# Packed small parameters, weights issued without a wait, and vectors requested later, in a three-block forward pass on one core

## The chip, the core and the metric

The kernel runs as one program on one core of one Trainium2 chip. The metric is the device time of one execution in microseconds (us); less is better. Three executions of the kernel before took 2320.06, 2322.34 and 2329.26 us: the median is 2322.34 us. One more execution was taken by the profiler: it took 2318.49 us, and its span, from the first to the last instruction of the trace, is 2316.6 us.

## What is computed

A sequence of 256 tokens of 1024 numbers, all in float32, passes through three blocks. The change touches the start of the first. Cut to that:

```python
cond = silu(c)
mod = cond @ w_mod + b_mod                      # (1, 6*1024)
sh1, sc1, g1, sh2, sc2, g2 = split(mod, 6)
h = layer_norm(x) * (1 + sc1) + sh1
z = h @ w_in + b_in                             # (256, 6*1024)
a_val, a_gate, sgu, g_a, g_b = split(z, ...)
ya = causal_conv31(a_val * sigmoid(a_gate), conv_w, conv_b)   # depthwise
ya = silu(layer_norm(ya) * ln_a_g + ln_a_b) @ w_a + b_a
u, v = split(gelu(sgu), 2)
yb = (u * (w_s_masked @ layer_norm(v) + b_s)) @ w_b + b_b     # w_s: 8 x 128 x 128
m = sigmoid(g_a) * ya + sigmoid(g_b) * yb
x = layer_norm(alpha * x + g1 * (m @ w_out + b_out)) ...
# then 32 experts with top-4 routing; then a retention and LRU block;
# then a gated linear attention and an S5 block
```

## The kernel before

**Engines and queues.** Each engine runs its own list of instructions in order, and semaphores join them. SyncE (SP) issues the transfers of all big weights. ScalarE (ACT) issues the small parameters and does activations and copies out of PSUM. GpSimd (POOL) issues vectors that are spread over all 128 partitions (`VECTORS`, L538) into two buffers `V`. VectorE (DVE) does norms, additions and the convolution. TensorE (PE) does matrix products and transposes.

**Weights.** All big matrices come in chunks of 1024 rows by 512 columns, 2 MB each, into a ring `W` of six buffers. `plan()` fixes the order: two chunks of `w_mod` for `sc1`, two for `sh1`, then `w_in` in the order ag0, av0, ag1, av1, v0, v1, u0 and so on. SP issues chunk n (L403) when chunk n-6 has been used up; the first six need no such wait.

**The start.** SP issues the constants `K` (L363), then `x` (L364), and then waits for all 19 parameter transfers (L366) and for `w_s` (L367) before the first weight. ACT meanwhile issues those 19 transfers one after the other into `PVR`, `LDT` and `BM` (L1261), and after them `w_s` into `WSR` (L1285). The parameters stand row by row there, so PE turns them with 5 transposes and `w_s` with 8 (helper `turn`, L679); ACT copies the results to `PC` (L1296 to L1301) and `WST` (L1306). ACT applies silu to the 8 columns of `c` (L1303), DVE spreads them to `CB` (L1682) and writes zeros over the masked quarter of `WST` (L1685). DVE then waits for `x` and forms mean, variance and, with a square root on ACT (L337), `RS` (L304 to L316).

**The modulation.** `mod_rows(name)` adds the bias rows `BM` (L649) and multiplies `CB` with each chunk of `w_mod` as it lands (L655). `copy_mod` on ACT copies the result to `MODROW` (L1315), and raises `mod_copied`. `mod_spread(name)` spreads it over all partitions in PSUM (L667). The order on PE is rows sc1, rows sh1, spread sc1, spread sh1. `modulated_norm` on DVE uses spread sc1 for (x - mean) * sc1 (L1695), then spread sh1 for the factor `RS` and the addition (L1703). PE turns the rows of h in 16 transposes over two alternating PSUM banks (L691), ACT copies each bank (`copy_columns`, L354), and then `dense("ag0")` starts (L604).

**After it.** ag and av are column products (L604), all later ones of this stage row products (L616). ACT forms sigmoids of ag (L1327), DVE multiplies (L1733) and runs the 31 steps of the convolution (L1720). The first spread vector is read when v0 and v1 are done (L1667). `WST` is first read by `mix(0)` (L738), after ga1.

The order around the change, on PE:

```python
pe.wait_ge(ev("cond_ready"), 1)
mod_rows("sc1")
mod_rows("sh1")
mod_spread("sc1")
mod_spread("sh1")
h1 = row(HN)
for t in range(TT):
    pe.wait_ge(ev("rows_ready"), NORMED["h1"] + t + 1)
    row_to_columns("h1", t, h1[:, t])
columns_ready("h1")
```

Of the kernel before, what the change touches and what calls it, by code (L numbers as in the profile page):

```python
# [18 lines left out]
ACT = mybir.ActivationFunctionType  # L19

P = 128
T = 256
TT = T // P
D = 1024
# [4 lines left out]
ROW = TT * D  # L29
# [23 lines left out]
R_C, R_AV, R_AG, R_CB, R_BS = 0, 8, 16, 24, 32  # L53
R_CW2, R_CB2, R_GAB, R_GXB, R_LAM, R_BG, R_GLU = 40, 72, 80, 88, 96, 104, 108
R_N0 = 124
N_PARAM = 19
# [89 lines left out]
TRANSPOSES = [("params", 2), ("ws", 2), ("h1", 4), ("yb", 4), ("conv", 4), ("ya", 4), ("m", 4), ("h2", 4),  # L146
# [13 lines left out]
def build(nc, A, out):  # L160
# [20 lines left out]
    with ExitStack() as ctx:  # L181
# [58 lines left out]
        def ev(name):  # L240
            if name not in S:
                S[name] = sem(name)
            return S[name]
# [118 lines left out]
        def _(sp):  # L362
            sp.dma_start(K[:], A["k_const"]).then_inc(const_landed, 16)  # L363
            sp.dma_start(X, A["x"][0].rearrange("(t p) d -> p t d", p=P)).then_inc(x_landed, 16)  # L364

            sp.wait_ge(param_landed, 16 * N_PARAM)  # L366
            sp.wait_ge(ev("ws_landed"), 16)  # L367
# [50 lines left out]
        WSR = half(GB, 0).rearrange("p (g i) -> p g i", g=8)  # L418
        PVR = BIG[:, CV * ROW:CV * ROW + 5 * P].rearrange("p (a b) -> p a b", a=5)
        LDT = BIG[:, CV * ROW + 5 * P:CV * ROW + 5 * P + 2]  # L420
# [112 lines left out]
        def _(pool):  # L533
            for n, (name, off, length) in enumerate(VECTORS):
# [55 lines left out]
        def _(pe):  # L590
# [95 lines left out]
            def row_to_columns(name, t, src):  # L686
                for h in range(2):
                    n = TB[name] + 2 * t + h
                    pe.wait_ge(tp_copied, n - 1)
                    for j in range(4):  # L690
                        ins = pe.transpose(PS[:, 4 + n % 2, j * P:(j + 1) * P], src[:, (4 * h + j) * P:(4 * h + j + 1) * P], ident)  # L691
                    ins.then_inc(tp_ready, 1)
# [19 lines left out]
            pe.wait_ge(param_landed, 16 * N_PARAM)  # L712
            pe.wait_ge(ev("log_dt_ready"), 1)
            turn("params", [[PVR[0:R_N0, 0, :], PVR[:, 1, :], PVR[0:120, 2, :], PVR[:, 3, :]], [PVR[0:80, 4, :]]])
            pe.wait_ge(ev("ws_landed"), 16)
            turn("ws", [[WSR[:, 4 * b + j, :] for j in range(4)] for b in range(2)])
            pe.wait_ge(ev("cond_ready"), 1)
            mod_rows("sc1")
            mod_rows("sh1")
            mod_spread("sc1")  # L720
# [529 lines left out]
        def _(act):  # L1250
# [9 lines left out]
            def param(dst, src):  # L1260
                act.dma_start(dst, src).then_inc(param_landed, 16)  # L1261

            def v128(a):
                return a.rearrange("(r q) -> r q", q=P)

            param(PVR[R_C:R_C + 8, 0, :], v128(A["c"][0]))
            param(PVR[R_AV:R_AV + 8, 0, :], v128(A["b_in"][0, 0:D]))
            param(PVR[R_AG:R_AG + 8, 0, :], v128(A["b_in"][0, D:2 * D]))
            param(PVR[R_CB:R_CB + 8, 0, :], v128(A["conv_b"][0]))
            param(PVR[R_BS:R_BS + 8, 0, :], A["b_s"][0])  # L1270
            param(PVR[R_CW2:R_CW2 + 32, 0, :], A["conv_w_2"].rearrange("j (k q) -> (j k) q", q=P))
            param(PVR[R_CB2:R_CB2 + 8, 0, :], v128(A["conv_b_2"]))
            param(PVR[R_GAB:R_GAB + 8, 0, :], A["gate_a_b_2"])
            param(PVR[R_GXB:R_GXB + 8, 0, :], A["gate_x_b_2"])
            param(PVR[R_LAM:R_LAM + 8, 0, :], v128(A["lru_lambda_2"]))
            param(PVR[R_BG:R_BG + 4, 0, :], v128(A["gla_b_gate_3"][0]))
            param(PVR[R_GLU:R_GLU + 16, 0, :], v128(A["s5_b_glu_3"][0]))
            param(PVR[:, 1, :], A["conv_w"][0, 0:16].rearrange("j (k q) -> (j k) q", q=P))
            param(PVR[0:120, 2, :], A["conv_w"][0, 16:31].rearrange("j (k q) -> (j k) q", q=P))
            param(PVR[0:64, 3, :], A["s5_lam_re_3"][0].rearrange("(a b) p -> a (b p)", b=2))  # L1280
            param(PVR[64:128, 3, :], A["s5_lam_im_3"][0].rearrange("(a b) p -> a (b p)", b=2))
            param(LDT[0:64], A["s5_log_dt_3"][0].rearrange("(a b) -> a b", b=2))
            param(PVR[64:80, 4, :], A["s5_d_3"][0].rearrange("(a b) i -> a (b i)", b=8))
            param(BM, v128(A["b_mod"][0]))
            act.dma_start(WSR, A["w_s"][0].rearrange("g i j -> i g j")).then_inc(ev("ws_landed"), 16)  # L1285

# [5 lines left out]
            for b in range(2):  # L1292
                act.wait_ge(tp_ready, TB["params"] + b + 1)
                n_ = 4 if b == 0 else 1
                if b == 0:
                    act.activation(PC[:, 0, 0:R_N0], PS[:, 4, 0:R_N0], ACT.Copy)  # L1296
                    act.activation(PC[:, 1, :], PS[:, 4, P:2 * P], ACT.Copy)
                    act.activation(PC[:, 2, 0:120], PS[:, 4, 2 * P:2 * P + 120], ACT.Copy)
                    act.activation(PC[:, 3, :], PS[:, 4, 3 * P:4 * P], ACT.Copy).then_inc(tp_copied, 1)
                else:  # L1300
                    act.activation(PC[:, 4, 0:80], PS[:, 5, 0:80], ACT.Copy).then_inc(tp_copied, 1)  # L1301
            act.drain()
            act.activation(pcol(R_C, 8), pcol(R_C, 8), ACT.Silu).then_inc(ev("silu_c_ready"), 1)  # L1303
            for b in range(2):
                act.wait_ge(tp_ready, TB["ws"] + b + 1)
                act.activation(WST[:, 4 * b:4 * b + 4, :], PS[:, 4 + b, :].rearrange("p (k t) -> p k t", k=4),  # L1306
                               ACT.Copy).then_inc(tp_copied, 1)
# [12 lines left out]
            copy_columns(act, "h1", col(HT))  # L1320
            sg = col(U)
# [341 lines left out]
        def _(dve):  # L1663
# [11 lines left out]
            for q in range(4):  # L1675
                dve.tensor_copy(SPREAD[:, q, :], ident[:, 32 * q:32 * q + 1].to_broadcast([P, P]))
            dve.drain()
            dve.wait_ge(param_landed, 16 * N_PARAM)
            dve.tensor_copy(PVR[0:64, 4, :].rearrange("p (b q) -> p b q", b=2),
                            LDT[0:64].unsqueeze(2).to_broadcast([64, 2, 64])).then_inc(ev("log_dt_ready"), 1)  # L1680
            dve.wait_ge(ev("silu_c_ready"), 1)
            dve.tensor_copy(CB, pcol(R_C, 8).unsqueeze(2).to_broadcast([P, KT, 32])).then_inc(ev("cond_ready"), 1)  # L1682
            dve.wait_ge(tp_copied, TB["ws"] + 2)

            dve.memset(WST[64:128, :, 0:64], 0.0).then_inc(ev("wst_ready"), 1)  # L1685
# [22 lines left out]
            modulated_norm(h1, X, "sc1", "sh1", ev("rows_ready"))  # L1708

# [661 lines left out]

# [18 lines left out]
```

## Time and profile before

| | us |
|---|---|
| median of three executions | 2322.34 |
| the profiled execution | 2318.49 |
| its span | 2316.6 |
| TensorE busy with matrix products | 2165.1 |
| VectorE busy | 751.5 |
| ScalarE busy | 468.7 |
| start of the first product with `w_in` (ag0) | 52.17 |

The times of the profile are counted from the start of the span. A busy share over the whole span mixes stages with different limits: the start, up to 52.17 us, is another stage than the one behind it. PE is the engine for products; its weight loads (PEld) lie beside them. Rows of the trace give the start, the duration, the engine (SPq, ACTq and POOLq are issues of transfers), the line, what is written and read, and in square brackets the idle time before it with what ended it. The granted TensorE clock is given as a share of the full 2.4 GHz, so 0.50 is 1.2 GHz.

### The profile page before, as it was taken

To read this page: it belongs to the slowest core of one execution; us is meant where nothing else is said; L and a number is where in the kernel's file an instruction comes from. 1 tells how busy PE (TensorE), PEld (TensorE's weight loads), DVE (VectorE), ACT (ScalarE), POOL (GpSimd) and SP (SyncE) were. 2 spreads that over 40 slices of the span, in tenths; PEclk is the share of its full clock that TensorE was granted. 3 is DMA by queue.
4 is the path that set the end of the run, shared out by engine and by line. 5 is a ranking of instruction groups with operands and counts; after the bars stand their busy time and mean duration, and the time that the engine had idled before them with its cause. 6 is when DMAs were issued, how large, how long until landed. Compare 5 with 4: busy or idle time off the path is not lost.

```text
span 2316.6 us, 30267 instructions
## 1 busy us (share of the span) xinstructions
PE 2165.1 (93%) x11523; PEld 1138.8 (49%) x11524; DVE 751.5 (32%) x1836; ACT 468.7 (20%) x930; POOL 65.4 (3%) x79
## 2 busy tenths in 40 slices
PE   5999998989999998999989998999999999999998
PEld 4844455343333333333333334844565446787873
DVE  1596234212222222222211223232212353988100
ACT  1011102111111111111110111131112215898100
POOL 0000000000000000000000000000000000222000
PEclk9999998999999999999999999999999999999999
DMA  9645557859999999999996799435133323232241
GB/s 345 223 163 181 209 196 285 337 224 417 418 418 418 418 418 381 418 417 418 417 383 265 317 417 384 148 112 200 68 141 133 123 103 125 74 110 74 103 164 42
DMA packets 158855, 591.31 MB, mean 255 GB/s; under 512 B 5323, under 2 KB 6927, under 8 KB 125887
## 3 DMA queue, kind: packets, MB, share of 16 engines
q1 hardware_dynamic: 152512, 573.08, 63.2%
q0 software_dynamic: 4384, 16.40, 2.0%
q8 instruction: 51, 0.84, 0.1%
q10 hardware_dynamic: 1887, 0.81, 0.1%
q14 instruction: 21, 0.17, 0.0%
HBM read 589.23 MB, written 1.05 MB: 255 GB/s over the span
## 4 chain that ended last, share of the span: by engine, by line
PE 74%; DMA 15%; DVE 5%; ACT 3%; DVEq 2%; issue 1%; ACTq 0%; SPq 0%
PE PS L616 22%; PE PS L922 13%; DMA W<-in_w_gu 13%; PE PS L604 10%; PE PS L945 6%; PE PS L1129 4%; PE PS L631 4%; PE PS L869 2%; PE PS L958 2%; PE PS L1202 1%; DVE BIG L1924 1%; PE PS L886 1%; DVE BIG L1928 1%; DMA W<-in_w_mod 1%; DVEq L1927 1%
## 5 line engine op out<-in xcount | busy, mean ns | idle before, releaser
L616 PE MATMUL PS<-W,BIG 128*128 128x512 f32 x1152 | 501.0, 596 | 5.0 <-DVE BIG L2358 2.9
L922 PE MATMUL PS<-W,BIG 128*64 128x512 f32 x2048 | 451.8, 595 | 21.0 <-DMA W<-in_w_gu 20.9
L616 PEld LDWEIGHTS PS<-W,BIG 128*128 128x128 f32 x1152 | 219.4, 191 | 277.2 <-issue 270.5
L922 PEld LDWEIGHTS PS<-W,BIG 128*64 128x64 f32 x2048 | 142.1, 137 | 313.0 <-issue 270.8
L945 PE MATMUL PS<-W,BIG 128*64 128x512 f32 x1024 | 228.8, 600 | 7.0 <-ACT BIG L1408 6.9
L604 PE MATMUL PS<-BIG,W 128*128 128x256 f32 x1024 | 222.2, 379 | 1.4 <-ACT BIG L354 1.4
L604 PEld LDWEIGHTS PS<-BIG,W 128*128 128x128 f32 x1024 | 194.2, 190 | 28.9 <-ACT BIG L354 1.9
L1922 DVE TENSOR_SCALAR BIG<-PS 128x512 f32<-128x512 f32 (+1 forms) x38 | 24.7, 650 | 379.6 <-PE PS L922 355.9
L945 PEld LDWEIGHTS PS<-W,BIG 128*64 128x64 f32 x1024 | 71.1, 138 | 144.0 <-issue 126.3
L1403 ACT ACTIVATE BIG<-BIG 128x512 f32<-128x512 f32 x32 | 20.2, 632 | 488.9 <-DVE BIG L1922 488.9
L1129 PE MATMUL PS<-BIG,W 128*128 128x256 f32 x512 | 118.3, 385 | 0.5 <-ACT BIG L1563 0.5
L1129 PEld LDWEIGHTS PS<-BIG,W 128*128 128x128 f32 x512 | 95.6, 192 | 15.6 <-issue 3.5
L1917 DVE COPY BIG<-PS 128x256 f32<-128x256 f32 x32 | 13.6, 425 | 260.1 <-PE PS L958 258.7
L1720 DVE SCALAR_TENSOR_TENSOR BIG<-BIG,PC 128x255 f32<-128x255 f32 (+29 forms) x240 | 95.4, 465 | 3.8 <-issue 0.5
L631 PE MATMUL PS<-W,BIG 128*128 128x512 f32 x192 | 82.9, 592 | 0.0
L827 PE MATMUL PS<-BIG 128*64 128x512 f32 x256 | 62.5, 610 | 4.3 <-issue 4.3
L1411 ACT ACTIVATE BIG<-PS 128x512 f32<-128x512 f32 x32 | 19.1, 598 | 232.1 <-PE PS L945 232.1
L958 PE MATMUL PS<-BIG 64*128 64x256 f32 x512 | 63.9, 389 | 0.8 <-ACT BIG L1411 0.8
L958 PEld LDWEIGHTS PS<-BIG 64*128 64x128 f32 x512 | 47.0, 186 | 30.9 <-issue 26.8
L631 PEld LDWEIGHTS PS<-W,BIG 128*128 128x128 f32 x192 | 36.5, 190 | 45.9 <-issue 45.9
L2111 DVE TENSOR_TENSOR X<-X,PS 128x512 f32<-128x512 f32 x12 | 8.0, 686 | 128.1 <-PE PS L631 67.5
L869 PE MATMUL PS<-W,BIG 128*32 128x256 f32 x768 | 45.6, 398 | 3.0 <-DVE BIG L1932 3.0
(460 smaller groups left out, 1963.2 us busy)
## 6 DMA issues: line engine op xcount, KB each, us to landing
W<-in_w_gu SPq DMA_DIRECT2D x128, 2048.0 KB, 17.3
W<-in_w_dn SPq DMA_DIRECT2D x64, 2048.0 KB, 19.1
W<-in_w_in SPq DMA_DIRECT2D x24, 2048.0 KB, 15.1
W<-in_w_mod SPq DMA_DIRECT2D x12, 2048.0 KB, 9.6
W<-in_gla_w_in SPq DMA_DIRECT2D x10, 2048.0 KB, 7.9
W<-in_s_w_in SPq DMA_DIRECT2D x8, 2048.0 KB, 8.9
W<-in_s_w_glu SPq DMA_DIRECT2D x8, 2048.0 KB, 8.0
W<-in_w_out SPq DMA_DIRECT2D x6, 2048.0 KB, 8.3
```

The source lines that it names most:

```text
L604: ins = pe.matmul(ps[:, m // 2, (m % 2) * T:(m % 2 + 1) * T], slot(c0 + i)[:, k, m * P:(m + 1) * P], lhs(i * KT + k), start=i + k == 0, st ...
L616: ins = pe.matmul(ps[:, t, :], lhs(i * KT + k)[:, t * P:(t + 1) * P], w[:, k, :], start=i + k == 0, stop=last_chunk and k == KT - 1)
L631: ins = pe.matmul(ps[:, t, :], lhs(i * KT + k)[:, t * P:(t + 1) * P], w[:, k, :], start=i + k == 0, stop=i == 1 and k == KT - 1)
L827: ins = pe.matmul(PS[hh[h], 3, :], G[:, t, :], H2[:, t, h * CH:(h + 1) * CH], start=t == 0, stop=t == TT - 1, skip_group_check=True)
L869: ins = pe.matmul(PS[qq[q], g, 0:T], XETX[:, k, :], gu_w(k)[:, g * D + q * T:g * D + (q + 1) * T], start=False, stop=k == KT - 1, skip_gro ...
L886: ins = pe.matmul(PS[qq[q], 2, T:2 * T], ACTTX[:, k, :], dn_w(k)[:, q * T:(q + 1) * T], start=k == 0, stop=k == KT - 1, skip_group_check=True)
L922: ins = pe.matmul(PS[hh[h], g, :], XET[:, k, :], gu_w(k)[:, g * D + h * CH:g * D + (h + 1) * CH], start=False, stop=k == KT - 1, skip_grou ...
L945: ins = pe.matmul(PS[hh[h], 2, :], ACTT[:, k, :], dn_w(k)[:, h * CH:(h + 1) * CH], start=k == 0, stop=k == KT - 1, skip_group_check=True)
L958: ins = pe.matmul(PS[:, 4 + q, t * T:(t + 1) * T], SC[r, t * P:(t + 1) * P], YE[r, (q % 2) * T:(q % 2 + 1) * T], start=False, stop=False, ...
L1129: ins = pe.matmul(PS[:, 5, part * T:(part + 1) * T], slot(c0)[:, k, m * P:(m + 1) * P], lhs(k), start=k == 0, stop=k == KT - 1, skip_group ...
L1720: ins = dve.scalar_tensor_tensor(cv[:, k, lag:], ya[:, k, 0:T - lag], pcol(r), cv[:, k, lag:], ALU.mult, ALU.add)
L1922: dve.tensor_scalar(GT[:, w], PS[:, 0, w], 7.0, None, ALU.min).then_inc(clipped, 1)
```

## The change

- The parameters are laid out on the host side in one array `k_params` of 128 x 640 numbers in the turned order that `PC` has (`log_dt` repeated 64 times). ACT issues three transfers: `PC`, `BM`, and `x`, which moves here from SP. The 18 small transfers, `PVR`, `LDT`, the 5 transposes, ACT's five copies and DVE's copy of `LDT` are gone.
- SP issues the weights right behind `K`, with no wait.
- `w_s` is laid out turned as well. ACT issues it straight into `WST`, behind the copies of h1. Its 8 transposes and two copies are gone. DVE waits for it behind `modulated_norm` and writes the zeros there.
- POOL waits for `mod_copied` 2 (sc1 and sh1 copied) before its first vector.
- PE spreads sc1 before the rows of sh1.

```diff
-            sp.dma_start(X, A["x"][0].rearrange("(t p) d -> p t d", p=P)).then_inc(x_landed, 16)
-
-            sp.wait_ge(param_landed, 16 * N_PARAM)
-            sp.wait_ge(ev("ws_landed"), 16)
...
         def _(pool):
+            pool.wait_ge(ev("mod_copied"), 2)
...
-            pe.wait_ge(param_landed, 16 * N_PARAM)
-            pe.wait_ge(ev("log_dt_ready"), 1)
-            turn("params", [[PVR[0:R_N0, 0, :], PVR[:, 1, :], PVR[0:120, 2, :], PVR[:, 3, :]], [PVR[0:80, 4, :]]])
-            pe.wait_ge(ev("ws_landed"), 16)
-            turn("ws", [[WSR[:, 4 * b + j, :] for j in range(4)] for b in range(2)])
+            pe.wait_ge(param_landed, 32)
             pe.wait_ge(ev("cond_ready"), 1)
             mod_rows("sc1")
+            mod_spread("sc1")
             mod_rows("sh1")
-            mod_spread("sc1")
             mod_spread("sh1")
...
-            param(PVR[R_C:R_C + 8, 0, :], v128(A["c"][0]))
...
-            param(BM, v128(A["b_mod"][0]))
-            act.dma_start(WSR, A["w_s"][0].rearrange("g i j -> i g j")).then_inc(ev("ws_landed"), 16)
+            act.dma_start(PC[:], A["k_params"].rearrange("p (a r) -> p a r", a=5)).then_inc(param_landed, 16)
+            act.dma_start(BM, A["b_mod"][0].rearrange("(r q) -> r q", q=P)).then_inc(param_landed, 16)
+            act.dma_start(X, A["x"][0].rearrange("(t p) d -> p t d", p=P)).then_inc(x_landed, 16)
...
+            act.wait_ge(param_landed, 32)
             act.activation(pcol(R_C, 8), pcol(R_C, 8), ACT.Silu).then_inc(ev("silu_c_ready"), 1)
...
             copy_mod("sc1")
             copy_mod("sh1")
             copy_columns(act, "h1", col(HT))
+            act.dma_start(WST, A["w_s"].rearrange("j (g i) -> j g i", g=8)).then_inc(ev("ws_landed"), 16)
...
-            dve.wait_ge(tp_copied, TB["ws"] + 2)
-
-            dve.memset(WST[64:128, :, 0:64], 0.0).then_inc(ev("wst_ready"), 1)
             dve.wait_ge(x_landed, 16)
...
             modulated_norm(h1, X, "sc1", "sh1", ev("rows_ready"))
+            dve.wait_ge(ev("ws_landed"), 16)
+
+            dve.memset(WST[64:128, :, 0:64], 0.0).then_inc(ev("wst_ready"), 1)
```

## Rows read from the trace of the kernel before

**Rows 1.** Busy time by stage: us, busy (instructions) of each engine, clock, DMA, GB/s

```profile
0.00:52.00 52.00, 25.18 (x333) 19.78 (x334) 10.35 (x25) 9.24 (x19) 1.46 (x6) 0.93 0.95 340
52.00:108.00 56.00, 55.83 (x258) 48.98 (x259) 26.61 (x66) 5.82 (x11) 0.00 (x0) 1.00 0.65 234
108.00:192.00 84.00, 84.00 (x209) 38.22 (x208) 80.10 (x185) 6.61 (x5) 2.12 (x4) 1.00 0.51 176
```

**Rows 2.** The chain that ended last, 0 to 60 us: start, duration, what

```profile
9.34 4.13 DMA BIG<-in_w_s
...
18.26 21.31 DMA W<-in_w_mod
...
39.61 1.96 PE PS L655 x64
41.57 1.94 PE PS L667 x8
...
46.34 0.75 DVE BIG L1703
...
47.80 3.69 PE PS L691 x16
...
51.52 0.61 ACT BIG L354
```

**Rows 3.** Timeline of the start: start, duration, engine, line, what, count

```profile
0.73 0.38 SPq L363 DMA_DIRECT2D K<-in_k_const  x1
...
16.53 0.29 DVE L1682 COPY BIG<-PC 128x256 f32<-128x256 f32 x1 [3.75 <-ACT PC L1303]
...
18.20 2.47 DVE L304 BATCH_NORM_STATS2 ST<-X 128x6 f32<-128x512 f32 x4
...
21.30 0.20 ACT L337 ACTIVATE SD<-VE 128x2 f32<-128x2 f32 x1 [2.49 <-DVE VE L309]
...
21.80 3.64 PE L655 MATMUL PS<-W,BIG 128*32 128x128 f32 x64 [4.28 <-DMA W<-in_w_mod]
...
27.23 3.62 PE L655 MATMUL PS<-W,BIG 128*32 128x128 f32 x64 [1.20 <-DMA W<-in_w_mod]
...
30.93 0.38 ACT L1315 ACTIVATE MISC<-PS 128x256 f32<-128x256 f32 x1 [9.42 <-PE PS L655]
...
34.19 3.56 PE L655 MATMUL PS<-W,BIG 128*32 128x128 f32 x64 [2.98 <-DMA W<-in_w_mod]
```

**Rows 4.** Transfers, 0 to 60 us: rate in 40 slices of 1.5 us, three issues

```profile
GB/s 0 242 378 387 316 330 293 195 162 31 255 412 406 386 389 386 385 388 388 393 386 389 384 388 386 389 389 386 388 384 386 389 385 388 389 384 388 385 386 388
...
X<-in_x SPq DMA_DIRECT2D x1, 1024.0 KB, 7.2
V<-in_b_in POOLq DMA_DIRECT2D x2, 512.0 KB, 8.3
K<-in_k_const SPq DMA_DIRECT2D x1, 528.0 KB, 3.4
```

**Rows 5.** Transfers from 13.5 to 39.6 us, all queues together

```profile
DMA packets 4666, 9.45 MB, mean 362 GB/s; under 512 B 64, under 2 KB 64, under 8 KB 4664
```

**Rows 6.** PE alone in short stretches: us, busy (instructions), clock, DMA, GB/s

```profile
34.10:35.50 1.40, 1.31 (x28) 0.51 1.04 383
...
41.50:43.50 2.00, 2.00 (x13) 1.00 1.06 389
47.70:48.70 1.00, 0.90 (x4) 0.54 1.04 383
```

**Rows 7.** Timeline: the next work of ACT and DVE, and V's first use

```profile
66.29 1.57 ACT L1327 ACTIVATE BIG<-PS,PC 128x256 f32<-128x256 f32 x4 [12.87 <-PE PS L604]
...
80.16 1.66 DVE L1733 SCALAR_TENSOR_TENSOR BIG<-PS,PC,BIG 128x256 f32<-128x256 f32 x4 [31.10 <-PE PS L604]
...
125.38 1.22 DVE L1667 TENSOR_TENSOR BIG<-PS,V 128x1024 f32<-128x1024 f32 x1
```

**Rows 8.** Line L538, all transfers of spread vectors: issue to landing

```profile
DMA to landing us min/median/max: 3.8/6.9/13.0
```

More of the change, by code:

```diff
@@ L55 @@
 R_N0 = 124
-N_PARAM = 19
 def constants():
@@ L142, in plan @@
     return units
-TRANSPOSES = [("params", 2), ("ws", 2), ("h1", 4), ("yb", 4), ("conv", 4), ("ya", 4), ("m", 4), ("h2", 4),
+TRANSPOSES = [("h1", 4), ("yb", 4), ("conv", 4), ("ya", 4), ("m", 4), ("h2", 4),
               ("xn", 4), ("q", 4), ("k", 4), ("yr", 4), ("hg", 4), ("kend", 1), ("og", 8), ("hs", 4)]
@@ L417, in build @@
         MODROW = MISC[:].rearrange("p (j c) -> p j c", c=T)
-        WSR = half(GB, 0).rearrange("p (g i) -> p g i", g=8)
-        PVR = BIG[:, CV * ROW:CV * ROW + 5 * P].rearrange("p (a b) -> p a b", a=5)
-        LDT = BIG[:, CV * ROW + 5 * P:CV * ROW + 5 * P + 2]
         MA, MB = half(9, 0), half(9, 1)
@@ L688, in row_to_columns @@
                     n = TB[name] + 2 * t + h
-                    pe.wait_ge(tp_copied, n - 1)
+                    if n >= 2:
+                        pe.wait_ge(tp_copied, n - 1)
                     for j in range(4):
@@ L1258, in half_copies @@
                                    PS[:, 4 + n % 2, :].rearrange("p (k t) -> p k t", k=4), ACT.Copy).then_inc(tp_copied, 1)
[L1260 to L1264, printed above, removed]
-            param(PVR[R_C:R_C + 8, 0, :], v128(A["c"][0]))
[L1267 to L1283, printed above, removed]
-            param(BM, v128(A["b_mod"][0]))
-            act.dma_start(WSR, A["w_s"][0].rearrange("g i j -> i g j")).then_inc(ev("ws_landed"), 16)
+            act.dma_start(PC[:], A["k_params"].rearrange("p (a r) -> p a r", a=5)).then_inc(param_landed, 16)
+            act.dma_start(BM, A["b_mod"][0].rearrange("(r q) -> r q", q=P)).then_inc(param_landed, 16)
+            act.dma_start(X, A["x"][0].rearrange("(t p) d -> p t d", p=P)).then_inc(x_landed, 16)
             def unit_act(name, dst, func, **kw):
@@ L1289, in unit_act @@
                 free_unit(act.activation(dst, unit_ps(name), func, **kw), name)
[L1292 to L1302, printed above, removed]
+            act.wait_ge(param_landed, 32)
             act.activation(pcol(R_C, 8), pcol(R_C, 8), ACT.Silu).then_inc(ev("silu_c_ready"), 1)
[L1304 to L1307, printed above, removed]
             act_std(act)
@@ L1677, in _ @@
             dve.drain()
-            dve.wait_ge(param_landed, 16 * N_PARAM)
-            dve.tensor_copy(PVR[0:64, 4, :].rearrange("p (b q) -> p b q", b=2),
-                            LDT[0:64].unsqueeze(2).to_broadcast([64, 2, 64])).then_inc(ev("log_dt_ready"), 1)
             dve.wait_ge(ev("silu_c_ready"), 1)
             dve.tensor_copy(CB, pcol(R_C, 8).unsqueeze(2).to_broadcast([P, KT, 32])).then_inc(ev("cond_ready"), 1)
-            dve.wait_ge(tp_copied, TB["ws"] + 2)
-            dve.memset(WST[64:128, :, 0:64], 0.0).then_inc(ev("wst_ready"), 1)
             dve.wait_ge(x_landed, 16)
@@ L2369, with packed, put @@
           "s5_b_im_3", "s5_c_re_3", "s5_c_im_3", "s5_d_3", "s5_w_glu_3", "s5_b_glu_3", "s5_w_out_3", "final_norm_3"]
+PACKED = ["c", "b_in", "conv_w", "conv_b", "b_s", "conv_w_2", "conv_b_2", "gate_a_b_2", "gate_x_b_2", "lru_lambda_2",
+          "gla_b_gate_3", "s5_b_glu_3", "s5_lam_re_3", "s5_lam_im_3", "s5_log_dt_3", "s5_d_3"]
+def packed(a):
+    rows = np.zeros((P, 5, P), np.float32)
+    def put(at, r, v):
+        v = np.reshape(v, (-1, P))
+        rows[r:r + v.shape[0], at] = v
+    put(0, R_C, a["c"])
+    put(0, R_AV, np.reshape(a["b_in"], -1)[0:D])
+    put(0, R_AG, np.reshape(a["b_in"], -1)[D:2 * D])
+    put(0, R_CB, a["conv_b"])
+    put(0, R_BS, a["b_s"])
+    put(0, R_CW2, a["conv_w_2"])
+    put(0, R_CB2, a["conv_b_2"])
+    put(0, R_GAB, a["gate_a_b_2"])
+    put(0, R_GXB, a["gate_x_b_2"])
+    put(0, R_LAM, a["lru_lambda_2"])
+    put(0, R_BG, a["gla_b_gate_3"])
+    put(0, R_GLU, a["s5_b_glu_3"])
+    put(1, 0, a["conv_w"][0, 0:16])
+    put(2, 0, a["conv_w"][0, 16:31])
+    put(3, 0, a["s5_lam_re_3"])
+    put(3, 64, a["s5_lam_im_3"])
+    put(4, 0, np.repeat(np.reshape(a["s5_log_dt_3"], (64, 2)), 64, axis=1))
+    put(4, 64, a["s5_d_3"])
+    return np.reshape(np.transpose(rows, (2, 1, 0)), (P, 5 * P))
 def kernel(**inputs):
@@ L2377 @@
     arrays, A = {}, {}
-    for name, a in [(n, inputs[n]) for n in INPUTS] + list(constants().items()):
+    laid = {n: inputs[n] for n in INPUTS if n not in PACKED or n == "b_in"}
+    laid.update(constants(), k_params=packed({n: np.asarray(inputs[n]) for n in PACKED}))
+    for name, a in laid.items():
+        if name == "w_s":
+            a = np.reshape(np.transpose(np.asarray(a)[0], (2, 0, 1)), (P, 8 * P))
         if name in ("s5_b_re_3", "s5_b_im_3"):
```

## The prediction

> **What bounds the kernel now.** I read the stages first [rows 1]. Behind 52 us TensorE is busy for 55.83 of 56 us and then for 84.00 of 84 us, while the transfers move 234 and 176 GB/s, well under the 386 to 393 of the start [rows 4]: from there on products set the pace, and nothing in this stretch counts from time zero. Before 52 us PE is busy for 25.18 of 52 us, most of it waiting. So the change is worth what it takes off the start of the first product, 52.17 us in the table, and everything behind it should move as one piece.
>
> Then the chain of waits of that start [rows 2]. It runs through the landing of `w_s` at 13.47 us (9.34 + 4.13), which frees SP to issue weights; through the weight stream up to 39.57 us; and through a tail of 12.6 us from there to 52.17: rows of the last chunk 1.96, spread sc1 1.94, DVE's first pass up to 46.34, half of its second pass 1.4 (46.34 to 47.80), transposes 3.69, the last copy 0.61. The timeline [rows 3] shows that the parameters' own work is no part of it beyond the issue: `CB` is ready at 16.82 us and the statistics are read from 18.20, while the first chunk lands only at 21.8.
>
> **Parts 1 and 2, parameters packed and weights at once: the last w_mod chunk lands earlier.** The parameters' issues go, and with them SP's wait. The bytes stay, and decide. The first bytes of `K`, issued at 0.73 us, come near 2.1 us: the slice from 1.5 to 3 moved 242 GB/s times 1.5 us = 0.36 MB, which is 0.94 us at 388 GB/s, a rate of many later slices [rows 3, 4]. What has to pass before the fourth chunk is in: `K` 0.54 MB, `PC` 128 x 640 x 4 = 0.33, `BM` 0.02, `x` 1.05, four chunks 8.39, together 10.33 MB. A transfer is not in when its own bytes' worth has moved, as later ones run beside it: between 13.5 us and the landing at 39.6 the queues moved 9.45 MB for those 8.39 [rows 5], so 1.06 MB more. I add the same: 11.4 MB at 388 GB/s = 29.4 us, so the fourth chunk lands at **31.4 us** against 39.57, 8.2 us earlier. Bounds: without the 1.06 MB it is 28.7; with twice as much, for two hardware queues where before was one, 34.1. I take the middle because it is the same stream through the same queue.
>
> The vectors (two times 0.5 MB) are out of that sum, since POOL now waits. It has only their issues in its queue, and the first reader is at 125.38 us [rows 7]; with the slowest landing of 13.0 us [rows 8] an issue near 34 lands by 47. So the wait costs nothing by itself. But they now run beside the chunk of ag0. That one lands 5.4 us behind the fourth (2.1 MB at 388), near 36.8; with 1.05 MB of vectors ahead of it, near 39.5. The first product wants it at 41.6 by the sum below: covered, by about 2 us. Without that cover it costs up to 2.7 us.
>
> The removed 13 transposes, 7 copies and DVE's one copy all lie before 21.8, on no path: nothing. The new path to `CB` is the landing of `PC`, silu, 0.29 us for `CB` [rows 3]. `PC` is a third of `x`'s size, and `x` took 7.2 us and `K` 3.4 [rows 4], so it lands between 4 and 9 us. The first chunk is in at 2.1 + (0.54 + 1.40 + 2.10 + 0.4)/0.388 = 13.5 us (with 0.4 MB more for what runs beside it, an estimate below the 1.06 of the fourth). `CB` is hidden, with 3 us or more to spare; later than 13.5 it would cost one for one only until PE catches up.
>
> **x behind the parameters on ACT.** DVE's statistics and the root take 3.3 us (18.20 to 21.5 [rows 3]), and ACT's square root stands in ACT's queue before the copy of sc1. That copy is wanted at about 22.6 us. The spread vectors, on a queue of their own beside SP's, took 13.0 us at most [rows 8]; by that `x`, issued near 1.8, lands by 15, and the root is done by 18.5. Hidden. The trace has no other case of a megabyte on ACT's queue, so this is the weakest cover; it is rival 2.
>
> First what the row shows: with three queues at work (SP, ACT, POOL) the total was 378 to 387 GB/s in the slices from 3 to 6 us, no more than the one queue's 388 later [rows 4]. A rule stands beside it that speaks against a part of this change: the Trainium skill, "DMA: Bandwidth & Descriptors", section "Issuing engines are not separate DMA queues", says that transfers from different engines end on the same 16 DMA engines and interleave, so that another issuer saves only its issuing time. By that rule `x` on ACT takes its 2.7 us from the weights, as my sum has it; if the queues added up, `PC` and `x` would cost nothing and the gain would be 3.6 us more.
>
> **Part 3, spread sc1 before rows sh1: a shorter tail.** The second chunk lands near 2.1 + (1.94 + 4.19 + 0.43)/0.388 = 19.0. Rows of a chunk take 3.64 us at the lower clock [rows 3], so they are done at 22.7, the copy (0.38 and two hand-overs, 0.5) at 23.2, the spread by 25.2 at the high clock (1.94) or 27.1 at the low one (twice that). The third chunk lands near 25.6, so its rows end at 29 to 31.3, ahead of the fourth. DVE does its first pass (2.8 us) meanwhile. So of the tail go 1.94 for spread sc1 and 2.8 for the first pass; what appears is what they hid: the copy of sh1 0.5 and spread sh1, about 1.85 (8 matmuls like spread sc1). New tail: 1.96 + 0.5 + 1.85 + 0.05 + 1.46 (half of the second pass) + 3.7 + 0.65 = 10.2 us against 12.6: **2.4 us** less. Bounds: 1.3 more if the transposes run at the high clock (below), and 3.5 less if the fourth chunk's rows and the spread still run at the low one (3.64 for 1.96, and 1.85 again).
>
> The clock is why these bounds stand. PE's 64 matmuls of a chunk took 3.6 us for each of the first three chunks [rows 3] and 1.96 for the fourth [rows 2]: 1.2 GHz, then 2.4. The granted clock reads 0.51 at 34.1 and 1.00 at 41.5 [rows 6]; before 34 the column reads 1.00, but the spacing of 57 ns is that of the lower level. It rose while PE was active with gaps of 1.2 to 3.3 us, and was down again at the transposes (0.54 at 47.7) behind an idle stretch of 2.6 us. In the new order PE works from 19 to 31 us with shorter gaps than before, thus the fourth chunk's rows should be at the high level as now. The gap before the transposes shrinks to 1.5 us. At the high level the 4 banks would go at the pace of ACT's copies, 0.45 + 4 x 0.65 = 3.05 us instead of 4.35: the 1.3 above. The Trainium skill, "TensorE: Matmul & The Clock Gate", section "The HAM clock gate", says that the array halves its rate after an idle stretch and that the point at which it changes varies from run to run; the trace's 0.54 behind 2.6 us of idling agrees. By that rule the shorter gap makes a fall less likely, and the sum would be the one with 1.3 more.
>
> **Part 4, w_s later.** Issued at about 41 us on ACT (0.6 us, next work of ACT before the change 14 us behind the start of ag0, [rows 7]), it lands within 4.1 [rows 2] to 13.0 us [rows 8], by 54 at the latest. DVE waits for it with the convolution queued behind; its next work stands 28 us behind the start of ag0, at 69.5 in the new time. The zeros take 0.5 us at most. `mix(0)` reads `WST` over 100 us later. Nothing. Without that cover each us of delay would go onto the convolution, which keeps DVE busy for 80.10 of 84 us [rows 1].
>
> **Sum.** 8.2 + 2.4 = 10.6 us, first product at about 41.6. Against the profiled execution: 2318.5 - 10.6 = 2307.9. That execution is 3.9 us below the median of the three; against the median it is 2322.3 - 10.6 = **2311.7 us**, 0.46% less. What is late next is the product chain itself.
>
> **Rivals.**
> 1. *The clock stays up over the transposes*: 11.9 us, 2310.4. For it: the gap of 1.5 instead of 2.6 us. Against it: the transposes of h1 are at the low level in the trace, though spread sc1 and spread sh1 just before them were at the high one.
> 2. *x is held behind the weights* (the other side). If ACT's queue got its turn only when SP's six chunks are through, `x` would land at 2.1 + (0.54 + 12.58 + 0.35 + 1.05)/0.388 = 39.5 us. Then statistics 3.3, root and copy of sc1 0.7, spread 1.94, both chunks' rows with their bias 4.8, copy 0.5, spread 1.85, and the end of the tail 5.9: first product at 58.5, 6.3 us later than now: 2328.6. It is slower than before once `x` lands after 33 us. Against it: POOL's vectors, on another queue than SP's, landed in at most 13.0 us beside full streams [rows 8]. The Trainium skill, the same DMA page, section "Queues, rings and completion order", says that each DMA engine takes turns between its queues; that agrees with this row.
> 3. *The landing slips, or the low clock stays*: twice the overshoot (2.7 us), the vectors beside ag0's chunk (up to 2.7), or the low clock in the last rows and the spread (3.5). Each alone leaves 7 to 8 us, two together 4 to 5: 2314.4 to 2318. For it: `w_mod`'s third chunk came 7.0 us behind the second (27.23 to 34.19 [rows 3]) where the others took 5.4, so such slips occur in this stream.
> 4. *The change does not reach the end*: the gain in the start is given back behind it, in a stage bound by transfers. Against it: no stage of rows 1 behind 52 us waits for a transfer that counts from zero. Time: 2318 to 2322.
>
> **How the numbers follow.** Forecast 45%, rival 1 25%, rival 3 20%, rival 2 5%, rival 4 5%. Three executions of before lie 9.2 us apart, so a median of three can be off by 2 to 3 us by itself. The range must leave 2 in 10 out: low, rival 1 with 4 us of scatter and a shorter landing (28.7 is 2.7 us below the forecast), 2305; high, rival 3 whole and 1 us of scatter, 2319. What a measurement can tell from no change is 0.5%, 11.6 us, just above the forecast's 10.6. So the forecast gives "faster" in about 4 cases of 10, rival 1 in 5.5 of 10, rival 3 hardly (0.18 + 0.14 + 0.02 = 0.34, some 0.38 with the possibility that the stream overshoots less); slower by 11.6 us is out of reach even of rival 2 (2%); the rest, 0.60, is within.
>
> **What would show it.** Right: the fourth chunk's rows at about 31.4 us, spread sc1 finished before they start, first L604 at 41 to 42, and every later stage the same length as before. `x`: statistics before 18 us. Part 3 is wrong if DVE's first pass still stands behind the fourth chunk; part 4 if DVE's line of the zeros waits past 69 us. The clock shows in the duration of the 64 matmuls (1.96 or 3.6) and of the transposes. The prediction is wrong above all if the product stages behind 52 us change their length, which the rows give no reason for.

## The result and the profile after

Five executions of the changed kernel have a median of 2305.66 us (2303.67 to 2306.96), five of the kernel before, on the same chip, 2320.31 us. The ratio is 0.993, with a 95% interval from 0.9913 to 0.9946: 14.7 us less by the medians, where the prediction said 10.6 and gave the larger chance, 0.60, to a change of less than 0.5%. The whole interval lies beyond 0.5%. The time is inside the range (2305 to 2319), at its lower edge.

The profiled execution of the changed kernel took 2306.96 us, the slowest of its five, and its span is 2304.8 us, 11.8 less than before. Its chain of waits at the start (start, duration, what; it answers to rows 2):

```profile
0.73 0.38 SPq L362
...
9.72 20.97 DMA W<-in_w_mod
30.69 0.04 issue
30.73 2.00 PE PS L648 x64
...
32.75 0.39 ACT MISC L1268
...
33.19 2.01 PE PS L660 x8
...
35.22 0.75 DVE BIG L1651
...
36.69 0.67 PE PS L685 x4
...
38.12 0.64 PE PS L685 x4
...
39.92 20.12 PE PS L597 x92
```

L648, L660, L1651, L685 and L597 are here what L655, L667, L1703, L691 and L604 were. The landing of `w_s` and DVE's first pass are no longer in the chain. The fourth chunk lands at 30.7 us instead of 39.6, and the first product starts at 39.92 instead of 52.17: 12.25 us earlier, 8.88 from the landing and 3.37 from the tail.

The timeline of the same stretch shows the work that the prediction held to be covered by other work (start, duration, engine, line, what, idle before; it answers to rows 3 and 7):

```profile
6.53 0.29 DVE L1633 COPY BIG<-PC 128x256 f32<-128x256 f32 x1 [1.05 <-ACT PC L1260]
...
10.99 2.47 DVE L303 BATCH_NORM_STATS2 ST<-X 128x6 f32<-128x512 f32 x4 [4.16 <-DMA X<-in_x]
13.19 3.64 PE L648 MATMUL PS<-W,BIG 128*32 128x128 f32 x64 [5.57 <-DMA W<-in_w_mod]
...
24.78 2.72 DVE L1643 SCALAR_TENSOR_TENSOR BIG<-X,MV,PS 128x512 f32<-128x512 f32 x4 [10.29 <-PE PS L660]
...
47.09 0.48 DVE L1659 MEMSET BIG<- 64x512 f32 x1 [9.15 <-DMA BIG<-in_w_s]
67.92 1.66 DVE L1684 SCALAR_TENSOR_TENSOR BIG<-PS,PC,BIG 128x256 f32<-128x256 f32 x4 [20.34 <-PE PS L597]
```

`CB` is ready at 6.8 us, 6 us ahead of the first chunk's rows. `x` has landed at 11, so the statistics are done long before the copy of sc1. DVE's first pass runs at 24.8, ahead of the fourth chunk. The zeros of `WST` end at 47.6, and DVE's next work is at 67.9.

Behind the start these two traces are alike. The products of ag and av take 55.52 us in both, and the first product of v0 starts at 95.44 against 107.69. From the first product to the end of the span it is 2264.9 us against 2264.4.

### The profile page after: what moved, and what is told of

It is laid out like the page before. It is cut to its first block, busy times and chain, and to the rows that moved or that the text cites. A ratio compares the mean times of both kernels' runs of the same rounds, so it can differ in the third digit from the quotient of the medians.

```text
span 2304.8 us, 30211 instructions
## 1 busy us (share of the span) xinstructions
PE 2159.5 (94%) x11510; PEld 1133.0 (49%) x11511; DVE 752.1 (33%) x1835; ACT 464.1 (20%) x922; POOL 65.4 (3%) x79
## 3 DMA queue, kind: packets, MB, share of 16 engines
HBM read 589.29 MB, written 1.05 MB: 256 GB/s over the span
## 4 chain that ended last, share of the span: by engine, by line
PE 74%; DMA 15%; DVE 5%; ACT 3%; DVEq 2%; issue 1%; SPq 0%; ACTq 0%
PE PS L609 22%; PE PS L912 14%; DMA W<-in_w_gu 13%; PE PS L597 10%; PE PS L935 6%; PE PS L1119 4%; PE PS L624 4%; PE PS L859 2%; PE PS L948 2%; PE PS L1192 1%; DVE BIG L1875 1%; PE PS L876 1%; DVE BIG L1879 1%; DMA W<-in_w_mod 1%; DVEq L1878 1%
## 5 line engine op out<-in xcount | busy, mean ns | idle before, releaser
L597 PE MATMUL PS<-BIG,W 128*128 128x256 f32 x1024 | 222.2, 379 | 1.5 <-ACT BIG L353 1.5
L597 PEld LDWEIGHTS PS<-BIG,W 128*128 128x128 f32 x1024 | 194.2, 190 | 29.0 <-ACT BIG L353 1.9
L1873 DVE TENSOR_SCALAR BIG<-PS 128x512 f32<-128x512 f32 (+1 forms) x38 | 24.7, 650 | 382.2 <-PE PS L912 356.5
```

Of the source, the lines that this page charges most:

```text
L597: ins = pe.matmul(ps[:, m // 2, (m % 2) * T:(m % 2 + 1) * T], slot(c0 + i)[:, k, m * P:(m + 1) * P], lhs(i * KT + k), start=i + k == 0, st ...
L1873: dve.tensor_scalar(GT[:, w], PS[:, 0, w], 7.0, None, ALU.min).then_inc(clipped, 1)
```

## The experiments

The kernel before ran 58 times beside them, on three chips with medians of 2320.1, 2320.3 and 2321.0 us: 2314.9 to 2329.0 us, median 2320.3. These executions differ more than the changes that I wanted to price, so a time below is read with its interval, and the trace of one execution of each kernel gives the places. "Landing" is the start of the fourth `w_mod` chunk's rows, "first product" the start of ag0. The low and the high level of the clock are 1.2 and 2.4 GHz; the 64 matmuls of a chunk's rows take 3.64 us at the one and 1.95 at the other, and a time between the two is a change on the way.

### The changed kernel again (r1_after_again)

No edit.

> The changed kernel again. The theory (the gain is the earlier start of the first product, 12.25 us in the first trace, and nothing behind it) expects a ratio of 0.9945 to 0.995, a difference of the medians of 11.5 to 12.5 us, and the first product again at 39.9 us. The rival (something behind the start gains 2 to 4 us more, which the first profiled pair happened not to show) expects a difference of 14 to 16 us, a ratio of 0.993 to 0.994.

Six executions: median 2309.06 us, ratio 0.9943 (0.9927 to 0.9959), 12.0 us less than the 2321.02 beside it. Together with the first five, eleven executions have a median of 2306.8 us, **13.5 us or 0.58% less** than the 58 of before. So the first ratio was a little lucky, and 10.6 a little short. The first product came at 41.60 and not at 39.9 as expected. The reason stands in PE's timeline and its stretches (us, busy, clock, DMA, GB/s):

```profile
30.77 3.62 PE L648 MATMUL PS<-W,BIG 128*32 128x128 f32 x64 [3.10 <-DMA W<-in_w_mod]
34.87 1.99 PE L660 MATMUL PS<-MISC,TAB 128*128 128x256 f32 x8 [0.48 <-ACT MISC L1268]
```

```profile
25.30:27.30 2.00, 1.94 (x68) 1.00 1.05 387
30.80:32.80 2.00, 2.00 (x40) 0.51 1.04 383
```

The landing is the same to 0.04 us. The clock had been at 2.4 GHz for the third chunk's rows and was at 1.2 for the fourth's, behind 3.10 us of waiting for weights; in the first trace it stayed up over 3.11 us of the same waiting. Of the traces with the new start (r1_after_again, c1_old_order, d1_pool_free, x1_x_first, h1_small_head and the first), five show the low level there, for all or most of it, with 3.3 to 3.6 us, and one 1.96. My sum had the high level; the low one stood in rival 3 only.

### Only SP's waits out (b1_weights_free)

```diff
-            sp.wait_ge(param_landed, 16 * N_PARAM)
-            sp.wait_ge(ev("ws_landed"), 16)
```

> The kernel before with SP's two waits ahead of the weights taken out, nothing else. If only bytes count, x, the parameters, w_s and the vectors (1.05 + 0.3 + 0.5 + 1.05 MB) now share the queues with the weights: fourth w_mod chunk at 2.1 + (12.0 + 0.7)/0.388 = 34.7 us, first product at about 47.3, 4.9 us earlier than 52.17. The rival, that the many small parameter transfers are held up beside full streams, expects the parameters complete only behind 20 us and a gain under 3 us.

Landing at 36.07 and first product at 48.32 us, 1.4 and 1.0 later than by bytes alone. Median of ten 2318.75, ratio 0.9983 (0.9970 to 0.9995). PE's timeline:

```profile
23.82 1.97 PE L677 MATMUL PS<-K,BIG 128*128 128x128 f32 x8 [5.65 <-DMA BIG<-in_w_s]
...
26.30 2.74 PE L653 MATMUL PS<-W,BIG 128*32 128x128 f32 x64
```

`w_s`, 0.5 MB, was issued at 9.55 us on ACT and landed at 23.8: 14.3 us beside SP's stream, where it took 4.1 without one [rows 2]. PE stood behind it with the first chunk landed (17.8 us by the trace of its transfer; the second came at 24.7, the third at 30.1), and caught up just before the fourth. So the rival about held-up small transfers has the mechanism right (the last parameter came at 16.6 instead of 12.5 us) but not the amount, as it expected 20. Taking the waits out alone is worth 3.9 us at the first product. The medians differ by 2.3 us only; ag and av took 57.26 us here and not 55.52, so that v0 starts 2.1 us earlier than in the first trace. The rest of the landing's gain is in the bytes taken out of its way.

### Spread sc1 behind the rows again (c1_old_order)

```diff
             mod_rows("sc1")
-            mod_spread("sc1")
             mod_rows("sh1")
+            mod_spread("sc1")
             mod_spread("sh1")
```

> The changed kernel with spread sc1 put back behind the rows of sh1. The fourth chunk should land at 30.7 us as before. If the order is worth spread and first pass (4.75 us less the 2.4 that they hid), the first product comes at 42.2 us with the transposes at the high clock, and at 43.5 if the longer idle stretch ahead of them brings the low clock back. The rival, that the order is worth nothing because PE keeps up anyway, expects 39.9.

Landing 30.82, first product 44.78 us; median of seven 2311.46, ratio 0.9954 (0.9938 to 0.9969). The chain (start, duration, what):

```profile
30.82 3.33 PE PS L648 x64
34.14 1.94 PE PS L660 x8
36.10 0.75 DVE BIG L1643
...
38.92 0.75 DVE BIG L1651
...
40.38 3.73 PE PS L685 x16
```

From the landing to the first product it is 13.96 us with 3.33 for the rows; r1_after_again had 10.83 with 3.62. Less the rows, that is 10.6 against 7.2: the order is worth **3.4 us**. Of them 1.2 are the clock (4.40 us from the first transpose to the first product, against 3.24). The 16 transposes take 3.73 us here behind an idle stretch of 2.6 us, as in the kernel before [rows 2], and run at the high level behind 1.5 us in the new order. The branch of the expectation with the low clock (43.5 us) was right, once the rows' 1.4 us are taken off.

### The new order alone (e1_order_alone)

```diff
             mod_rows("sc1")
+            mod_spread("sc1")
             mod_rows("sh1")
-            mod_spread("sc1")
```

The kernel before with this edit only.

> The kernel before with only the order on PE changed: spread sc1 ahead of the rows of sh1. The fourth chunk should land at 39.6 us as before. With the transposes at the low clock the first product comes at 50.1 us, with them at the high clock (as the changed kernel showed, behind a gap of 1.5 us) at 48.8; 52.2 if the order is worth nothing. The time 2 to 3.5 us below that of before.

Landing 39.45, first product 49.98 us with 2.59 and 2.76 us for rows and spread of sh1 (the granted clock was 0.88 up to 41 us, 0.50 from there into the spread and 0.98 at the spread's end, so it fell within the rows and rose again), and transposes at the high level. Median of ten 2314.73, ratio 0.9970 (0.9958 to 0.9982): 5.5 us less, where the trace's first product is only 2.2 earlier than in the first trace of before. This is the first sign of something that a single pair of traces does not show.

### POOL's wait out (d1_pool_free)

```diff
         def _(pool):
-            pool.wait_ge(ev("mod_copied"), 2)
```

> The changed kernel without POOL's wait, so that the two spread vectors (1.05 MB) are requested at 1.2 us again. If only bytes count, the fourth chunk lands 2.7 us later, at 33.4, and the first product at 42.6. The rival, that a third queue fits beside the others, expects the landing at 30.7 and the first product at 39.9.

Landing 34.20 us, first product 45.00; median of five 2311.91, ratio 0.9960 (0.9941 to 0.9980). 1.05 MB of vectors move the landing by 3.4 us, more than their bytes at 388 GB/s (2.7); why more is not shown. A third queue brought nothing of its own. So POOL's wait, which the prediction's sum assumed and gave no price of its own, is worth 3.4 us of the landing's 8.9.

### x first on SP (x1_x_first)

```diff
             sp.dma_start(K[:], A["k_const"]).then_inc(const_landed, 16)
+            sp.dma_start(X, A["x"][0].rearrange("(t p) d -> p t d", p=P)).then_inc(x_landed, 16)
...
-            act.dma_start(X, A["x"][0].rearrange("(t p) d -> p t d", p=P)).then_inc(x_landed, 16)
```

> The changed kernel with x back on SP, between K and the first weight chunk. If only bytes count, the fourth chunk lands at 30.8 us again and the first product comes at 39.9 to 41.6 as in the two traces of the changed kernel; only the first chunk comes later, by up to 2 us, which PE's slack hides. The rival, that ACT's queue gave x a way beside SP's stream, expects the landing 2.7 us later, at 33.5.

Landing 30.82, first product 41.32 us (rows 3.31), median of five 2309.30, ratio 0.9959 (0.9945 to 0.9973). Which queue carries `x` makes no difference to the landing, which r1_after_again has at 30.77: bytes count, as rows 4 had suggested. The Trainium skill, "DMA: Bandwidth & Descriptors", section "Issuing engines are not separate DMA queues", says the same: transfers from different engines interleave on the same 16 DMA engines. The two landings agree with it, 30.82 and 30.77 us.

### x last (g1_x_last)

```diff
+                    if n == 5:
+                        sp.dma_start(X, A["x"][0].rearrange("(t p) d -> p t d", p=P)).then_inc(x_landed, 16)
```

and `x` taken off ACT's queue: rival 2 made by hand.

> The changed kernel with x issued by SP behind the first six weight chunks: the prediction's rival 2 made by hand. x should land near 2.1 + (0.54 + 0.35 + 12.58 + 1.05 + 0.8)/0.388 = 41.6 us, and the first product come 19 us behind it, at 60.6; the fourth chunk then lands 2.7 us earlier, at 28. The time would be 20 us over that of the changed kernel, so 5 to 8 us over before. If statistics, root, copy and spread cost less than the sum has it, the first product comes at 55 or earlier.

```profile
24.41 17.14 DMA X<-in_x
41.58 0.69 DVE ST L304
...
45.21 3.78 PE PS L663 x8
...
61.43 2.64 PE PS L600 x11
```

`x` landed at 41.55 us and the first product came at 61.43, against 41.6 and 60.6 expected. Median of ten 2328.59, ratio 1.0033 (1.0021 to 1.0044): slower than before, by 8.3 us. From the landing of `x` to the first product it was 19.9 us, where the rival had 19.0; the rival's total of 6.3 us was short, mostly because `x` lands 2 us later here than its 39.5. That the median is the rival's 2328.6 to the tenth is luck: the rival counted from 2322.3, and before ran at 2320.3. So the rival's path was right and its price nearly so, and what kept it away was that the queues share: on ACT's queue, beside the weights, `x` took 9.3 us.

### Clock held in the old order (f1_clock_kept)

```diff
             mod_spread("sh1")
+            keep_active(4, 10)
             h1 = row(HN)
```

The kernel before with 10 matmuls of no use (20 instructions in the trace), which `keep_active` sends to a free PSUM bank.

> The kernel before with 10 matmuls of no use (identity times identity into a PSUM bank that is free) behind spread sh1, which fill PE's idle stretch of 2.6 us. If that stretch is what brings the low clock to the transposes of h1, these take 2.2 us instead of 3.7, bound by ACT's copies, and the first product comes at 50.9 us. If the clock falls for another reason, 52.2 and 3.7 as before.

As a price for the transposes this failed. In the traced execution the clock was low for the fourth chunk's rows (3.64 us) and the added matmuls (4.3 us) ended some 1.6 us after DVE's rows were ready, so the first product came at 54.27. The transposes did run at the high level. The median of ten tells more: 2317.75, ratio 0.9977 (0.9967 to 0.9988), 2.5 us less than the kernel before with more work in the chain. ag and av took 55.52 us. That keeping PE active there saves time in the first product too is likely by the next section, but one trace of the slower half does not show it.

### The kernel before, twice more (p1_before_again, p2_before_third)

> The kernel before again, for a second trace. If the scatter of its executions (2317.5 to 2329.0 us) is in where the clock rises in the start, the first product comes at another time than 52.17 us, up to 2 us later. If it is behind the start, the first product comes at 52.2 again and the stretch from there to the end differs from 2264.4 us.

> The kernel before once more, for a third trace of where its executions differ. The first two traces had the 256 matmuls of ag and av in 55.5 and in 57.5 us (the second began at the low clock), and their first at 52.17 and 53.35. The theory that the start's clock is chance expects either pair again or one between: v0's first product between 107.7 and 110.9 us.

2324.48 and 2322.86 us. First product at 53.35 and 51.58, v0's at 110.85 and 109.08: 57.50 us for the matmuls of ag and av in both, not 55.52. PE's timeline of the first of these:

```profile
49.29 1.09 PE L691 MATMUL PS<-K,BIG 128*128 128x128 f32 x8 [2.59 <-DVE BIG L1703]
50.73 1.94 PE L691 MATMUL PS<-K,BIG 128*128 128x128 f32 x8 [0.34 <-ACT BIG L354]
53.35 57.49 PE L604 MATMUL PS<-BIG,W 128*128 128x256 f32 x256 [0.69 <-ACT BIG L354]
```

Stretches of the second (us, busy, clock, DMA, GB/s), first the transposes, then ag0:

```profile
48.80:51.00 2.20, 1.94 (x8) 0.50 1.05 385
51.50:54.00 2.50, 2.42 (x6) 0.50 1.05 385
54.00:56.00 2.00, 2.00 (x7) 0.60 1.05 386
56.00:58.00 2.00, 2.00 (x11) 1.00 1.05 384
```

The clock fell only between the first and the second eight transposes (1.09 and 1.94 us), and the low clock reaches some 4 us into the first product and costs 2.0 us there. In the first trace of before and in c1_old_order it was low for the 16 together (3.69 and 3.73 us) and was up again when the first product began. So the low stretch behind these 2.6 us of idling is paid at one of two places. b1_weights_free had it as the two new traces (0.50 from 48.3, and 57.26 us for ag and av). So of the six traces with the old order three pay 2 us (the first trace, on which the prediction rested, c1_old_order and f1_clock_kept do not), and of the eight with the new order none: 55.52 in each. The old order makes it possible, not certain; if both orders were alike in this, such a split would still come up about once in 18.

With this the two kernels compare well: v0's product starts at 107.69, 110.85 and 109.08 in the three traces of before (mean 109.2) and at 95.44 and 97.12 in the two of the changed kernel (mean 96.3). That is **12.9 us**, beside 13.5 between the medians. The spans of the same traces differ by 14.5 (2320.1 and 2305.6 on average), so here another 1.6 us lies behind v0.

Behind v0, too, executions of one kernel differ. p1_before_again is 6.1 us slower than the first trace, 3.2 of them up to v0 and 2.9 behind; in b1_weights_free the first expert's 64 matmuls at 386 us take 15.69 us, not 13.88 (p2_before_third has 15.79), and the stage from v0 on is 6 us longer than in the first trace. Over the 58 executions of before, those with a mean granted clock of 0.984 took 2314.9 to 2318.5 us and those with 0.979 took 2325.8 to 2329.0. The eleven of the changed kernel had 0.983 to 0.985.

### A smaller head (h1_small_head)

```diff
-            sp.dma_start(K[:], A["k_const"]).then_inc(const_landed, 16)
+            sp.dma_start(K[:, 0:T], A["k_const"][:, 0:T]).then_inc(const_landed, 16)
...
             act.dma_start(WST, A["w_s"].rearrange("j (g i) -> j g i", g=8)).then_inc(ev("ws_landed"), 16)
+            act.dma_start(K[:, T:C_N], A["k_const"][:, T:C_N]).then_inc(ev("ws_landed"), 16)
...
-            dve.wait_ge(ev("ws_landed"), 16)
+            dve.wait_ge(ev("ws_landed"), 32)
```

> The changed kernel with only the first 256 of the 1056 columns of K ahead of the weights; the other 0.41 MB are requested on ACT behind w_s. By bytes the fourth chunk lands 0.41/0.388 = 1.1 us earlier, at 29.7, and the first product comes at 38.8 (40.5 if the fourth chunk's rows run at the low clock).

Landing 30.07, first product 40.85 us with rows at the low clock (3.58). Beside r1_after_again that is 0.7 us earlier at both places; 1.1 was expected. Median of four 2308.56, ratio 0.9950 (0.9933 to 0.9967), not to be told from the changed kernel.

### The same, with PE kept active (i1_kept_active)

```diff
+KEEP = (12, 2, 0, 6)
...
+                    if j < 2:
+                        keep_active(4, KEEP[2 * j + i])
                     pe.wait_ge(w_landed[slot_no(n)], load_count(n))
...
             mod_spread("sh1")
+            keep_active(4, 5)
```

> The same with matmuls of no use in PE's idle stretches of the start: 12 ahead of the first chunk's rows, 2 ahead of the second's, 6 ahead of the fourth's, 5 behind spread sh1. If the clock is what differs between executions of the changed kernel in the start (1.96 or 3.64 us for the fourth chunk's rows), all of it now runs at the high level: first product at 38.8 us, executions within 3 us of each other, and a median 1 to 3 us under that of h1. The rival, that where the clock rises is chance that such matmuls don't change, expects 3.64 us again and no difference from h1.

Here `keep_active` fills PE's idle stretches of the start. PE's timeline (L703 is the added work):

```profile
26.93 2.86 PE L703 MATMUL PS<-K 128*128 128x256 f32 x12
30.07 1.95 PE L651 MATMUL PS<-W,BIG 128*32 128x128 f32 x64 [0.29 <-DMA W<-in_w_mod]
32.53 1.99 PE L663 MATMUL PS<-MISC,TAB 128*128 128x256 f32 x8 [0.51 <-ACT MISC L1272]
34.36 2.32 PE L703 MATMUL PS<-K 128*128 128x256 f32 x10
36.52 1.04 PE L688 MATMUL PS<-K,BIG 128*128 128x128 f32 x8
```

All four chunks' rows now take 1.95 us, and the first product comes at 39.70 us, 0.9 later than 38.8: the landing is 0.4 later than expected, and the last 10 instructions end at 36.68, where the rows of h1 should have been ready near 36.0, which costs the other 0.5. Median of six 2304.65 us, ratio 0.9931 (0.9917 to 0.9946), 2.1 us below the median of the changed kernel's eleven and 3.9 below h1. The intervals overlap, so it is likely the best of these kernels, not shown to be. The expected narrowing to 3 us failed: 2300.8 to 2302.6 in three, 2306.7 to 2308.6 in three. The traced one is of the slower half (2308.6), with the first expert's matmuls at the low clock:

```profile
375.65 15.56 PE PS L916 x64
```

In this trace the added work has settled the start; the other executions have no trace. The entry of the experts is another place where the clock differs between executions: of the fourteen traces four have it low there (b1_weights_free, f1_clock_kept, p2_before_third and this one), the others 13.88 us.

## Why the prediction was partly right and where it failed

**The step that failed.** The forecast of less than 0.5% rested on a gain of 10.6 us, just under the 11.6 that are 0.5%; 14.7 were measured, and 13.5 over all executions. The path was right and its terms too small. What failed is the clock in the sum: the transposes with the last copy were taken at the low level, 4.35 us, and took 3.23; and the first product was taken to cost the same before and after, where two further traces of before pay 2.0 us for the low clock in it. The landing was 0.7 us short besides. The rest of the 14.7, about 1.7 us, is in no term: the second set of executions gave 12.0, with an interval (0.9927 to 0.9959) that does not lie wholly beyond 0.5%. So how clearly the first five came out beyond 0.5% is partly luck.

**What bounds the start: right.** In the profiled pair the gain came off the time before the first product and nothing behind it changed its length. Over more traces this holds but for the low clock at the start of ag0 (below) and the 1.6 us behind v0, of which the runs do not show whether they come from the change.

**Landing of the fourth chunk: right within 0.7 us, 30.73 for 31.4.** (The prediction's own numbers add up to 31.5.) The four landings were 13.2, 18.6, 25.3 and 30.7 against 13.5, 19.0, 25.6 and 31.4. The count of bytes with 1.06 MB for what runs beside was a little high. x1_x_first and d1_pool_free show the rule behind it: total bytes ahead at 388 GB/s, whichever queue they are in (the vectors cost more, 3.4 for 2.7).

**Cover by parameters, x, w_s and vectors: right.** `CB` at 6.8, the statistics at 11.0, `w_s` landed at 47.0, ag0's chunk in time (its releaser is ACT's copy). The price of a late `x` was nearly right as well (g1_x_last).

**The tail: the terms that hold no clock were right, the clock was not.** Without it, copy 0.5, spread 2.0 for 1.85, half a second pass 1.46, hand-overs: as summed. Three terms with a clock failed, and they are why the sum was short:

- *Transposes, 4.35 us with the last copy, taken at the low level.* They ran at the high one in every trace of the new order, behind a gap of 1.5 us (filled in i1_kept_active): 3.23 us from 36.69 to 39.92. This was rival 1, with 25%; the size (3.05 forecast) was about right, the choice wrong. 1.15 us. In two of the three traces of before the transposes themselves were low only for the second half, and the clock's other cost lay in the next term.
- *The first product, 0 us.* The step "everything behind it should move as one piece" took the 55.52 us of one trace as the kernel's own. Two further traces of before have 57.50. On average of the three that is 1.3 us which no trace of the new order pays, and it was in no term and no rival.
- *The fourth chunk's rows, 1.96 us, "should be at the high level as now".* They were at the low one in five of six traces. This goes the other way, 1.65 us whenever it happens; in the profiled trace it did not, in r1_after_again it did. The prediction had it in rival 3.

The sum of the profiled pair is then 10.6 + 0.7 + 1.15 - 0.15 (spread) = 12.3, the 12.25 measured. For the average of the kernels, 12.3 less about 0.8 (rows low in one of the changed kernel's two traces) plus 1.3 for the clock in ag0, and 0.2 because the first product of before comes at 52.4 on average and not at 52.17, gives 13.0, against 12.9 by the traces of v0 and 13.5 by the medians. The agreement with 12.9 is bookkeeping, as both come from the same five traces; the 13.5 is the independent number.

**Rival 3 looked only to one side.** It spoke of the landing slipping and the low clock staying as losses from the forecast. Its evidence, the third chunk 7.0 us behind the second, was no slip: the rows stand 6.7 and 6.8 us apart in the two traces of the changed kernel as well, and the sum had 6.6. Nothing was said of before itself paying for its clock more often than its one trace showed. There was a hint: the traced execution was 3.9 us under the median of the three. I wrote that down as scatter and took the gain off the median unchanged, which supposes that both kernels scatter alike.

**What stays open.** Where exactly the clock rises or falls between executions of one kernel: r1_after_again and the first trace have idle stretches equal to 0.01 us ahead of the fourth chunk and different levels behind them. What PE did earlier differed (2.00 us of idling ahead of the third chunk's rows against 0.22), but x1_x_first, with next to none there, has the low level as well. The 0.6 us between 12.9 and 13.5, and the 1.6 behind v0, are within what two and three traces can tell. Not tried alone were the packing and the later `w_s`: the landing's 8.9 us split by the runs into 3.5 (SP free, b1_weights_free: 39.61 to 36.07), 3.5 (vectors, d1_pool_free: 34.20 to 30.73) and the last 1.9, for which `w_s` is 0.52/0.388 = 1.35 by estimate. The remaining half microsecond may be the packed parameters; no run shows it.

## What to carry to other kernels

In a start that waits for weights, count every byte that is requested before the last needed one, on whichever queue, and move what has a late reader behind it: the wait in front of the vectors was worth as much as the earlier issue of the weights. A short wait of TensorE can cost more than its own length: behind 2.6 us of idling the low clock fell on the transposes or reached into the first long product. Take work that can be done earlier out of such a tail, so that the wait gets shorter, or fill the gap. And where executions of a kernel differ by more than the expected gain, read two or three traces of it before a term is called zero.

## What the runs showed of the hardware

- The granted clock stood at 1.00 in one execution and 0.51 in another behind equal idle stretches of 3.1 us. Mean clock and time go together over 58 executions of one program: 0.984 with 2314.9 to 2318.5 us, 0.979 with 2325.8 to 2329.0.
- A transfer of 0.5 MB on ACT's queue took 4.1 us with no weights in flight and 14.3 us beside SP's weights (b1_weights_free); `x`, 1 MB, took 9.3 us there (the changed kernel). The streams share, none is held to the end.
- Behind 2.6 us of idling the clock was low for 16 transposes in two traces (3.7 us for all, first product at the high level) and fell after the first four to eight of them in three (1.1 to 1.3 us for eight, then 1.94, and the first product low for its first 3.5 to 4 us). Behind 1.5 us of idling it stayed up in the seven traces that have this gap.
- With twelve instructions of useless matmul work in a gap of 3.1 us, and more of it in the gaps before, the rows behind them took 1.95 us for 64 matmuls in the one trace (i1_kept_active), where five of six traces without them had 3.3 to 3.6.
